# First mixer's input projection on rows that are not yet divided by their root mean square; the row factor enters where results leave PSUM

## What is computed

```
def rmsnorm(x, g):
    y = x * rsqrt(mean(x * x, axis=-1) + 1e-6)     # one factor a row
    return y * g                                   # one gain a column

y = rmsnorm(h, norm_g[0, 0])
proj = y @ w_in                    # 256 x 1024 @ 1024 x 3608, layer 0
q, k (rotated by rope), v, gates = sigmoid(part of proj), ...
```

## Time and profile before

| | |
|---|---|
| median of 3 runs | 680.04 us (679.62 to 681.54) |
| the profiled execution's own time | 681.87 us |
| its span in the profile | 680.1 us |
| PE busy | 658.4 us, 97% of the span |
| DVE, ACT, POOL busy | 460.6, 379.4, 153.4 us |
| chain that ended last, share of PE | 91% |
| moved by DMA | 116.20 MB, mean 171 GB/s |

### The profile page before, as it was taken

How to read it: one execution, slowest core, us unless ns; L and a number is a source line. 1 busy time by engine, 2 the same in 40 slices (tenths; PEclk the granted TensorE clock), 3 DMA queues, 4 the chain that set the end, 5 groups by cost and what they waited for, 6 DMA issues and landing times.

```text
span 680.1 us, 10214 instructions
## 1 busy us (share of the span) xinstructions
PE 658.4 (97%) x3719; PEld 549.0 (81%) x3719; DVE 460.6 (68%) x618; ACT 379.4 (56%) x539; POOL 153.4 (23%) x117
## 2 busy tenths in 40 slices
PE   4999999899999999999999999999999999999996
PEld 3888877668788888888887999777788888888885
DVE  4586776796678787877446654575776878786532
ACT  5556435684667676766345533575476666667320
POOL 0121220000024444443001000381122434343000
PEclk9999999999999999999999999999999999999999
DMA  8957643004263636364642754302355363635601
GB/s 334 404 195 289 202 177 124 1 3 153 94 248 123 238 133 246 124 239 189 253 186 96 276 185 187 124 1 107 142 194 208 130 241 128 242 130 184 243 1 62
DMA packets 18651, 116.20 MB, mean 171 GB/s; under 512 B 2463, under 2 KB 3133, under 8 KB 5693
## 3 DMA queue, kind: packets, MB, share of 16 engines
q1 hardware_dynamic: 17325, 111.52, 43.8%
q10 hardware_dynamic: 1296, 4.26, 1.7%
HBM read 114.72 MB, written 1.05 MB: 170 GB/s over the span
## 4 chain that ended last, share of the span: by engine, by line
PE 91%; DVE 3%; issue 2%; ACT 2%; POOL 1%; DMA 1%; DVEq 0%; POOLq 0%; ACTq 0%
PE ps L1543 22%; PE ps L1161 13%; PE ps L1163 13%; PE ps L1162 13%; PE ps L1545 11%; PE ps L1203 6%; PE ps L1156 1%; PE ps L1322 1%; PE ps L1442 1%; PE ps L1594 1%; PE ps L1583 1%; POOL rstd L1076 1%; ACT xn L361 1%; DMA h<-in_x 1%; PE ps L1300 1%
## 5 line engine op out<-in xcount | busy, mean ns | idle before, releaser
L640 DVE TENSOR_TENSOR wlo<-raw,whi 128x2048 fp32r<-128x2048 f32 x99 | 225.9, 2312 | 64.3 <-ACT whi L338 64.0
L1543 PE MATMUL ps<-xpair,whi 128*128 128x512 f32 x640 | 226.4, 399 | 0.0
L338 ACT CAST whi<-raw 128x2048 fp32r<-128x2048 f32 x99 | 186.0, 1916 | 71.2 <-PE ps L1163 66.9
L1545 PE MATMUL ps<-xpair,wlo 128*128 128x256 f32 x640 | 179.7, 281 | 0.0
L1543 PEld LDWEIGHTS ps<-xpair,whi 128*128 128x128 f32 x640 | 120.3, 188 | 29.9
L1545 PEld LDWEIGHTS ps<-xpair,wlo 128*128 128x128 f32 x640 | 120.9, 189 | 0.0
L1116 POOL TENSOR_TENSOR hidf<-act_g,conv 128x512 f32<-128x512 f32 x22 | 74.0, 3362 | 83.8 <-ACT act_g L544 83.8
L1163 PE MATMUL ps<-whi,hid_lo 128*128 128x512 f32 x176 | 69.4, 394 | 0.0
L1162 PE MATMUL ps<-wlo,hid_hi 128*128 128x512 f32 x176 | 69.4, 394 | 0.0
L1161 PE MATMUL ps<-whi,hid_hi 128*128 128x512 f32 x176 | 69.4, 394 | 0.0
L1161 PE MATMUL ps<-whi,xpair 128*128 128x512 f32 x168 | 68.2, 406 | 1.0 <-DVE pcm L832 0.8
(11 more groups left out here) (173 smaller groups left out, 962.5 us busy)
## 6 DMA issues: line engine op xcount, KB each, us to landing
raw<-in_weights SPq DMA_DIRECT2D x101, 1024.0 KB, 5.0
c_gpre<-in_gpre ACTq DMA_DIRECT2D x4, 512.0 KB, 4.7
raw<-in_weights SPq DMA_DIRECT2D x4, 512.0 KB, 8.3
c_gpost<-in_gpost ACTq DMA_DIRECT2D x4, 512.0 KB, 4.8
h<-in_x SPq DMA_DIRECT2D x2, 512.0 KB, 7.7
out<-h SPq DMA_DIRECT2D x4, 256.0 KB, 2.0
t<-in_masks SPq DMA_DIRECT2D x1, 512.0 KB, 14.2
c_rope<-in_rope SPq DMA_DIRECT2D x1, 256.0 KB, 14.1
```

The source lines that it names most:

```text
L338: act.copy(whi[:, slot, :], raw[:, slot, :]).then_inc(hi_done, 1)
L640: dve.tensor_tensor(wlo[:, slot, :], raw[:, slot, :], whi[:, slot, :].bitcast(F32), ALU.subtract).then_inc(lo_done, 1)
L1543: pe.matmul(ps[:, b0 + m, :], whi[:, slot, cols], xpair[:, kt].rearrange("p a c -> p (a c)"), start=kt == 0, stop=kt == KT - 1, skip_group ...
L1545: ins = pe.matmul(ps[:, b0 + m, 0:SEQ], wlo[:, slot, cols], xhi[:, kt, :], start=False, stop=kt == KT - 1, skip_group_check=True)
```

## The change

Both tiles of rows go to PE as they come from memory. The identity is built on POOL instead of loaded. Turned blocks get the gain as one number a partition (`c_gcol`, 4 KB) while they are split: for blocks 0 to 3 of tile 0 one by one, each in its own PSUM bank, in ACT's copy and DVE's subtraction; for the other twelve blocks by a multiplication of four on DVE that writes `xn`. The square sums stand after that, on ACT. The factor `rstd` enters where results leave PSUM: as ACT's scale in the copies to `xn` and `vbuf` (each copy of two tiles becomes one for each tile), as the scale of `Tanh`, and, for queries and keys, in the rotation tables, which POOL multiplies by it once. Unit 0 is loaded in pieces of 512, 512 and 1024 numbers a partition, and the rows of tile 1 before unit 1. PE has 13 products of zeros that nobody reads, 8 at the start and 5 after the first blocks are turned.

```diff
@@ sync
-            for u in range(HALVED):
-                for i in range(2):
-                    sp.dma_start(raw[:, u, uhalf(i)], weights[u, :, uhalf(i)]).then_inc(first_in[2 * u + i], 16)
-            sp.dma_start(h[:, 1, :], x[P:2 * P, :]).then_inc(x_in[1], 16)
+            for i in range(len(PIECES)):
+                u, cols, done = piece_of(i)
+                sp.dma_start(raw[:, u, cols], weights[u, :, cols]).then_inc(first_in[i], 16)
+                if u == 0 and done:
+                    sp.dma_start(h[:, 1, :], x[P:2 * P, :]).then_inc(x_in[1], 16)
@@ scalar
-            load_gain(c_gpre, gpre, 0, gpre_in)
-            act.dma_start(c_identf[:], identf).then_inc(ident_in, 16)
+            act.dma_start(c_gcol[:], gcol).then_inc(gcol_in, 16)
+            def row_block_hi(k):
+                if k == 0:
+                    act.wait_ge(gcol_in, 16)
+                    act.wait_ge(pre_tr, 1)
+                act.activation(xhi[:, k, 0:P], ps[:, ROW_BANK[k], 0:P], ACT.Identity,
+                               scale=c_gcol[:, k:k + 1]).then_inc(row_hi, 1)
+            def row_half_hi(t, c):
+                act.wait_ge(row_gain, 2 * t + c)
+                act.copy(xhi[:, 4 * c:4 * c + 4, t * P:(t + 1) * P],
+                         xn[:, t, colhalf(c)].rearrange("p (k c) -> p k c", c=P)).then_inc(row_hi, 1)
...
+            def values_out(v0, bank, c0, c1):
+                for t in range(TT):
+                    ins = act.activation(vbuf[:, t, v0:v0 + c1 - c0], ps[:, bank + t, c0:c1], ACT.Identity,
+                                         scale=rstd[:, 0, t:t + 1])
+                ins.then_inc(in_free_act, 1)
...
-                    act.activation(gates[:], ps[:, 4, 0:TT * NSA_HEADS * BRANCH].rearrange("p (t c) -> p t c", t=TT),
-                                   ACT.Tanh, scale=0.5).then_inc(gate_tanh, 1)
+                    act.wait_ge(half_rstd, 1)
+                    n = NSA_HEADS * BRANCH
+                    for t in range(TT):
+                        ins = act.activation(gates[:, t, :], ps[:, 4, t * n:(t + 1) * n], ACT.Tanh, scale=rstdh[:, t:t + 1])
+                    ins.then_inc(gate_tanh, 1)
@@ vector
+            def row_half_gain(t, c):
+                dve.wait_ge(pre_tr, 2 * t + c + 1)
+                dve.tensor_tensor(xn[:, t, colhalf(c)].rearrange("p (k c) -> p k c", c=P),
+                                  ps[:, T_BANK[0] + 2 * t + c, :].rearrange("p (k c) -> p k c", c=P),
+                                  c_gcol[:, 4 * c:4 * c + 4].unsqueeze(2).to_broadcast([P, 4, P]),
+                                  ALU.mult).then_inc(row_gain, 1)
+            row_block_lo(0)
+            row_block_lo(1)
+            split_piece(0)
+            split_piece(1)
+            row_block_lo(2)
+            row_block_lo(3)
+            row_half_gain(0, 1)
+            split_piece(2)
+            row_half_lo(0, 1)
+            row_half_gain(1, 0)
+            split_piece(3)
+            row_half_gain(1, 1)
+            row_half_lo(1, 0)
+            split_piece(4)
+            row_half_lo(1, 1)
             pre_ms_of(0, 0)
...
@@ gpsimd
+            pool.memset(c_mask[:, 0:2, :], 0.0).then_inc(warm_set, 1)
             pool.memset(mhalf[:], -0.5).then_inc(half_set, 1)
+            pool.memset(c_identf[:], 0.0).then_inc(ident_zero, 1)
             pool.wait_ge(half_set, 1)
+            pool.wait_ge(ident_zero, 1)
+            pool.affine_select(c_identf[:], c_identf[:], [[-1, P]], ALU.not_equal, 1.0, base=0,
+                               channel_multiplier=1).then_inc(ident_set, 1)
...
+            for t in range(TT):
+                pool.tensor_scalar(c_rope[:, :, :, t, :], c_rope[:, :, :, t, :], rstd[:, 0, t:t + 1], None,
+                                   ALU.mult).then_inc(rope_set, 1)
@@ tensor
+            def keep_warm(count):
+                zeros = c_mask[:, 0:2, :].rearrange("p m c -> p (m c)")
+                for _ in range(count):
+                    pe.matmul(ps[:, 7, 0:3 * P], zeros[:, 0:P], zeros[:, 0:3 * P], start=True, stop=True)
...
-            pe.wait_ge(ident_in, 16)
-            pre(0, 0)
+            pe.wait_ge(warm_set, 1)
+            keep_warm(8)
+            pe.wait_ge(ident_set, 1)
+            rows_turned(0)
+            keep_warm(5)
...
-                        first_units(u - 1, 0)
+                        row_units()
```

More of the change, by code:

```diff
@@ L170, in build @@
         raw_in = [sem(f"raw_in{s}") for s in range(RING)]
-        first_in = [sem(f"first_in{i}") for i in range(4)]
+        first_in = [sem(f"first_in{i}") for i in range(len(PIECES))]
         first_hi, first_lo = sem("first_hi"), sem("first_lo")
@@ L491, in _ @@
                     act.wait_ge(rope_parts, TT * 5)
-                    act.copy(vbuf[:, :, 512:768], ps[:, 2:4, 256:512]).then_inc(in_free_act, 1)
+                    values_out(V_DIL, 2, 256, BLK)
                 elif step == ("unit", 6, 1):
@@ L502, in _ @@
                     act.wait_ge(unit_used, EVEN_END["unit", 6])
-                    act.copy(vbuf[:, :, 768:1280], ps[:, 6:8, :]).then_inc(in_free_act, 1)
+                    values_out(V_DIL + 256, 6, 0, BLK)
                 if n < NI:
@@ new lines, in row_units, with products, kts_of, high @@
+            def row_units():
+                def products(x, w, kts, t, start=False, stop=False):
+                    for kt in kts:
+                        u, b = kt // 4, kt % 4
+                        ins = pe.matmul(ps[:, t, :], x[:, kt, t * P:(t + 1) * P], w[:, u, b * BLK:(b + 1) * BLK],
+                                        start=start and kt == kts[0], stop=stop and kt == kts[-1])
+                    return ins
+                def kts_of(i):
+                    u, b0, b1 = PIECES[i]
+                    return range(4 * u + b0, 4 * u + b1)
+                def high(i):
+                    kts = kts_of(i)
+                    if piece_of(i)[2]:
+                        pe.wait_ge(hi_done, PIECES[i][0] + 1)
+                    else:
+                        pe.wait_ge(first_hi, pieces_until(i))
+                    pe.wait_ge(row_hi, min(kts[-1] + 1, ROW_T0))
+                    products(xhi, whi, kts, 0, i == 0)
+                    pe.wait_ge(row_lo, min(kts[-1] + 1, ROW_T0))
+                    products(xlo, whi, kts, 0)
+                def low(i):
+                    if piece_of(i)[2]:
+                        pe.wait_ge(lo_done, PIECES[i][0] + 1)
+                    else:
+                        pe.wait_ge(first_lo, pieces_until(i))
+                    products(xhi, wlo, kts_of(i), 0, stop=i == len(PIECES) - 1)
+                for i in range(2):
+                    high(i)
+                    low(i)
+                high(2)
+                rows_turned(1)
+                low(2)
+                high(3)
+                pe.wait_ge(row_hi, ROW_T1)
+                products(xhi, whi, range(0, 4), 1, True)
+                products(xhi, wlo, range(0, 4), 1)
+                low(3)
+                pe.wait_ge(row_lo, ROW_T1)
+                products(xlo, whi, range(0, 4), 1)
+                high(4)
+                low(4)
+                pe.wait_ge(row_hi, ROW_T1 + 1)
+                products(xhi, whi, range(4, 8), 1)
+                products(xhi, wlo, range(4, 8), 1)
+                pe.wait_ge(row_lo, ROW_T1 + 1)
+                products(xlo, whi, range(4, 8), 1, stop=True).then_inc(unit_used, 2)
```

149 lines of the change are left out of this document (95 added, 54 removed).

## The result

The change takes the median from 679.97 us (679.62 to 681.54, 4 runs) to 675.04 us (674.93 to 676.46, 4 runs): 4.93 us less, a ratio of 0.9916 with a 95% interval of 0.9895 to 0.9936. The forecast was 676.0. The size is close, but it is made of other terms than the forecast's: less in the head, and something in the feed-forward stages that the forecast didn't have.

The account below looks back on a forecast made before the run. PE, busy 97% of a 680.1 us span, was taken as the bound. The gate's products starting 4.3 us earlier, less 0.3 for pick-ups, gave 680.04 - 4.0 = 676.0 us; range 674.4 to 679.4.

Parts of the forecast that it names:

- The rival with a late identity: At the start: library load takes 6.3 us, PE starts on rows at 8.4, gate at 25.2; 679.8 us, chance 0.14.
- the slower case built on it: At the start: load 6.3 us and select 3.36, identity at 11.3, kernel loses 2.5 us; 682.5 us, chance 0.04.
- The path from ACT's copy of unit 2 to the gate: Before the gate's products: unit 2's copy 1.9 us, DVE's subtraction 2.3, DVE's part of the gate weights 0.35.
- The rival with a PE at low clock: Up to the gate: products take 0.43 us until 14 us, gate at 23.6; 678.2 us, chance 0.12.
- Weights of unit 4: Behind the gate's start: arrive some 1.4 us earlier, wanted 4.3 us earlier, yet closing without a wait.
- ACT's list: ACT's work from 5.6 us to unit 2: items of 10.2 us plus 1.0 of waits, so unit 2 starts at 16.8.
- the head: Start to the gate's products: these begin at 21.4 instead of 25.75, 4.3 us earlier, 4.0 after 0.3 for pick-ups.
- The line of 1 us a 256 KB: First loads: each further 256 KB costs 1 us at most, two small pieces there by 6.6, the next by 8.6.
- issue of two gain loads, 0.8: Among ACT's work before unit 2: issuing two gain loads costs 0.33 + 0.45 us, counted as 0.8.
- The wait for DVE: Before unit 2: DVE reaches its last gain multiplication's end at 13.3, ACT is there at 12.3, so ACT waits 1.0 us.
- What it gains at 25.75 should reach the end: Behind the gate's start: PE has no gap until 80 us, so the gain reaches the end if weights follow.
- What moves without a price: Unpriced parts: six half-size `vbuf` copies, POOL's scaled tables perhaps 1 us, split `Tanh` 0.2 us, gains on DVE, unit 4's weights.

Follow-up runs that it names:

- the last kernel: The changed kernel with unit 0 in two pieces of 512 KB and 64 unused bytes more, putting `hid_hi` at 167296; 673.60 us, ratio 0.9894.

## Why the prediction was right or wrong

**Right.** The rows land at 4.37 and PE turns them from 4.50, forecast 4.55. That they land earlier without the gain beside them is borne out: 4.08 to 4.42 in all kernels with the new order, 5.48 to 5.99 in all with the old. The identity is there at 1.75 + 0.29 = 2.04 (forecast 2.5), 2.3 us ahead of the rows. The rows of before bounded the library load by 0 and 6.3 us; all idle time ahead of the select is 0.31. The rival with a late identity, and the slower case built on it, fall with that. ACT's first block is at 5.70, forecast 5.6. The path from ACT's copy of unit 2 to the gate takes 22.09 - 17.55 = 4.54 us, forecast 4.6. The rival with a PE at low clock falls as well: full clock came at 6.2 us, and the run without products of zeros shows that even 12.8 would have cost no more than 0.2. Weights of unit 4 do close without a wait of PE, but not for the reason given. They were to come "some 1.4 us earlier" and land at 27.77 instead of 25.09; ACT and DVE wait for them, behind PE's work:

```profile
23.45 2.48 POOL L1190 TENSOR_SCALAR c_rope<-c_rope,rstd 128x256 f32<-128x256 f32 x2 [4.37 <-DMA c_pe<-in_pe]
...
27.79 1.91 ACT L360 CAST whi<-raw 128x2048 fp32r<-128x2048 f32 x1 [3.20 <-DMA raw<-in_weights]
...
29.73 2.29 DVE L700 TENSOR_TENSOR wlo<-raw,whi 128x2048 fp32r<-128x2048 f32 x1 [5.49 <-ACT whi L360]
```

The same rows hold one size that was off at no cost: POOL's two scalings of tables, "perhaps 1 us", take 2.48.

**Mis-sized: ACT's list.** "So ACT starts on unit 2 at 5.6 + 10.2 + 1.0 = 16.8" came out at 17.55. Its waits are 0.51 + 0.20 + 1.02 + 0.42 = 2.15 us and not 1.0. Two of the four, both for transfers, I had not counted, and the one of 1.02 is the head's new bound. The line of 1 us a 256 KB, which I laid through the first three pieces only ("the next by 8.6"), gives 10.6 for tile 1's rows and 12.6 for unit 1's first piece when it is carried on; they landed at 10.34 and 12.21, and ACT was ready for the piece at 12.24 - 1.02 = 11.2. The working was at hand and stopped two transfers early. In the other direction, "issue of two gain loads, 0.8" is no part of the list: the rows at 15.20 and 15.58 run in ACT's queue while its copy at 15.18 and the sums behind it run on. What is left of the list is 17.55 - 5.70 - 2.15 = 9.70, against 10.2. The wait for DVE was right in kind and 0.20 + 0.42 = 0.62 in size; its 1.0 came from ACT "there at 12.3", where the items up to that copy add up to 6.9 us and so to 12.5.

**Mis-sized: the head.** PE was through at 21.8 and not "20.2 to 20.5" (the terms given for it, 6.9 to 7.3 and 13.0, add up to 19.9 to 20.3), since it waited for the same piece; it was still ahead of DVE, by 0.31 us instead of 1. The gate at 22.09 instead of 21.4, and 25.59 as its true first start before where the chain of waits puts 25.75, make 3.5 us at the gate and 3.43 behind it, for a forecast of 4.0.

**Half of a reason.** The forecast credited the gain's 512 KB to the rows alone. The bytes count for the weights as well: sent behind the rows instead of beside them they leave the rows where they are and delay the gate by up to 2.4 us. In the changed kernel itself the weights gained nothing by their absence in the end: unit 2 lands at 15.94 us, before at 15.89. With unit 0 in two pieces it lands at 14.45 and, in the last kernel, at 15.14.

**The step that failed: what the change moves.** "What it gains at 25.75 should reach the end" is right, but the list of the change's parts, "What moves without a price" with it, ended with instructions and bytes to load, and the place of the buffers stood at nothing without a reason. It moves the feed-forward's buffers by 64 bytes too, and this is worth 1.8 us, over a third of the whole gain. Nothing in the profile of before shows it as a wait; PE is simply busy in both. The sum with the parts as measured is 3.43 + 1.80 = 5.2 where the forecast said 4.0 + 0. That the forecast came within 1 us of the median is luck in part: a head taken 0.6 too large stood in for a third of a shift that was taken as nothing.

## What to carry to other kernels

When a transfer is taken out of the start or cut into pieces, carry the landing times on through the queue until the consumer's list is ahead again, not just through the first pieces. When a transfer is put back as a test, look whether it moves at the same time as before, and not just the same bytes. When a difference grows evenly over a stretch in which the bounding engine never waits, compare its step, instruction for instruction, and look at where the program put the operands: a small tensor that a change adds can move everything behind it. And test that part by itself with unused bytes in the kernel before, else it is booked as a gain of the change.

## What the runs showed of the hardware

- The step of products with a stationary operand of 128 x 128 float32 and 512 moving columns went from 0.2269 to 0.2334 us with the byte at which `hid_hi` begins: 0.2269 at 128 modulo 256, 0.2289 at 64, 0.2324 at 0, 0.2334 at 32.
- Two pieces of 256 KB and one of 512 KB at the start moved 229 and 355 GB/s in the stretches from 3.5 and 5.5 us, two pieces of 512 KB 308 and 406, at nearly the same busy share of the DMA engines (0.95 and 0.99 against 1.02 and 1.01). In the first stretch all five kernels with the small pieces stay under 230 and both with the large ones above 300; in the second the two kinds overlap.
- The first operation of POOL behind its library load started 0.31 us after the memset ahead of it. The GPSIMD Engine Reference of the Trainium skill, section Instruction dispatch, gives about 6 us for the first call to a freshly loaded kernel; this trace doesn't show them.
- A stretch of 3.4 us at half clock stands near 100 us, near 440 or at both in nine of fourteen profiled executions and costs some 1.6 us: 11 products started in four us instead of 26.
- 512 KB of rows landed at 5.48 to 5.99 us with 512 KB of gain issued beside them from another queue (six kernels), and at 4.08 to 4.42 without it or with it behind a small transfer of its own queue (eight).
